# One layer's query projections moved into hyena as whole fp32 tiles, and four modulation blocks moved into the state chain

## What is computed

```python
def adaln(cond, w, b):                       # "modulation": 6 x 1024 outputs per layer
    return (silu(cond) @ w + b).reshape(cond.shape[0], 6, D_MODEL)

proj = u @ w_in                              # hy_in, s_z, s_xbc, s_dt, a_q, a_k, a_v, g
z = x1 * long_conv(v, filt[0]); hy = x2 * long_conv(z, filt[1])      # hyena: FFT convolutions
h = d * h + s                                # state-space branch: the chain of states over chunks
att = softmax(rope(q) @ rope(k).T + mask, sink) @ v                  # banded attention, 8 heads of 64
merged = sigmoid(g0)*(hy @ hy_proj) + sigmoid(g1)*(ssm @ ssm_proj) + sigmoid(g2)*(att @ attn_proj)
x = x + m2 * rmsnorm(merged @ w_out); x = x + m5 * rmsnorm(ffn(...))
```

## Time and profile before

| | |
|---|---|
| time, median of 3 runs | 2896.82 us (2895.7 to 2900.62) |
| the profiled execution's own time, its span | 2894.71 us, 2892.9 us |
| PE, PEld | 2675.1 us (92%), 2314.2 us (80%) |
| DVE, ACT, POOL | 1252.3 us (43%), 801.5 us (28%), 264.3 us (9%) |
| mean granted TensorE clock | 0.960 |
| chain that ended last, by engine | PE 81%, DVE 12%, ACT 4%, issue 2% |
| 1 MB weight load, issue to landing | 5.1 to 5.4 us, median of its kind |
| 64 KB load of a q block | 2.1 us |

### The profile page before, as it was taken

How to read it: one execution, slowest core, us unless ns; L and a number is a source line. 1 busy time by engine, 2 the same in 40 slices (tenths; PEclk the granted TensorE clock), 3 DMA queues, 4 the chain that set the end, 5 groups by cost and what they waited for, 6 DMA issues and landing times.

```text
span 2892.9 us, 38685 instructions
## 1 busy us (share of the span) xinstructions
PE 2675.1 (92%) x16849; PEld 2314.2 (80%) x16849; DVE 1252.3 (43%) x1978; ACT 801.5 (28%) x1234; POOL 264.3 (9%) x174
## 2 busy tenths in 40 slices
PE   6989897889999899999988998788999998999998
PEld 4946445679999799999977564385899988999997
DVE  3495646452233422223356756636422343223224
ACT  5222122352224522112252211224321244221212
POOL 0020412000111000000001204210001110000000
PEclk8989998899999999999999999988999999999999
DMA  6021003223323032323302010122232221222221
GB/s 241 19 78 44 29 15 90 73 75 117 96 81 102 17 104 88 103 93 98 91 30 78 4 59 15 44 75 75 80 124 89 83 78 41 77 66 81 69 88 41
DMA packets 214622, 213.42 MB, mean 74 GB/s; under 512 B 29480, under 2 KB 205040, under 8 KB 214070
## 3 DMA queue, kind: packets, MB, share of 16 engines
q1 hardware_dynamic: 214454, 210.95, 23.2%
HBM read 207.52 MB, written 3.41 MB: 73 GB/s over the span
## 4 chain that ended last, share of the span: by engine, by line
PE 81%; DVE 12%; ACT 4%; issue 2%; POOL 1%; DMA 1%; SPq 0%; DVEq 0%; ACTq 0%
PE ps L622 54%; PE ps L581 6%; DVE arena L1614 4%; PE ps L605 3%; PE ps L1100 3%; PE ps L593 3%; PE ps L672 1%; PE ps L882 1%; DVE arena L1715 1%; PE ps L1010 1%; ACT normed L723 1%; DVE normed L748 1%; PE ps L1165 1%; PE ps L1260 1%; ACT arena L2081 1%
## 5 line engine op out<-in xcount | busy, mean ns | idle before, releaser
L622 PE MATMUL ps<-arena_parts,weights_parts 128*128 128x320 f32 x8416 | 1428.9, 309 | 3.6 <-DVE normed_parts L1689 3.6
L622 PEld LDWEIGHTS ps<-arena_parts,weights_parts 128*128 128x128 f32 x8416 | 1275.8, 187 | 19.2 <-DVE normed_parts L1689 4.4
L539 DVE TENSOR_TENSOR weights_parts<-weights,weights_parts 128x2048 fp32r<-128x2048 f32 (+2 forms) x140 | 285.5, 2039 | 772.5 <-ACT weights_parts L531 772.5
L622 PE MATMUL ps<-normed_parts,weights_parts 128*128 128x320 f32 x2240 | 510.0, 309 | 0.0
L622 PEld LDWEIGHTS ps<-normed_parts,weights_parts 128*128 128x128 f32 x2240 | 376.1, 188 | 0.0
L531 ACT CAST weights_parts<-weights 128x2048 fp32r<-128x2048 f32 (+2 forms) x140 | 232.5, 1660 | 267.8 <-PE ps L622 171.5
L581 PE MATMUL ps<-normed,weights 128*128 128x320 f32 x768 | 214.9, 439 | 6.2 <-DVE arena L1597 5.5
L581 PEld LDWEIGHTS ps<-normed,weights 128*128 128x128 f32 x768 | 146.2, 192 | 77.2 <-issue 20.5
L605 PE MATMUL ps<-arena_parts 128*128 128x320 f32 x448 | 104.8, 340 | 51.8 <-DVE arena_parts L755 19.8
L605 PEld LDWEIGHTS ps<-arena_parts 128*128 128x128 f32 x448 | 81.1, 209 | 60.4 <-DVE arena_parts L755 27.4
L2280 POOL TENSOR_TENSOR arena<-arena 128x640 f32<-128x640 f32 x32 | 54.4, 1699 | 787.6 <-DVE arena L1789 783.2
(11 more groups left out here) (261 smaller groups left out, 2586.3 us busy)
## 6 DMA issues: line engine op xcount, KB each, us to landing
weights<-in_w_in_dram SPq DMA_DIRECT2D x48, 1024.0 KB, 5.3
weights<-in_ada_w_dram SPq DMA_DIRECT2D x40, 1024.0 KB, 5.4
weights<-in_ffn_w_gate_dram SPq DMA_DIRECT2D x22, 1024.0 KB, 5.3
weights<-in_ffn_w_up_dram SPq DMA_DIRECT2D x22, 1024.0 KB, 5.3
weights<-in_ffn_w_down_dram SPq DMA_DIRECT2D x24, 768.0 KB, 4.4
weights<-in_w_out_dram SPq DMA_DIRECT2D x8, 1024.0 KB, 5.1
weights<-in_w_in_dram SPq DMA_DIRECT2D x66, 64.0 KB, 2.1
arena<-in_ada_w_dram SPq DMA_DIRECT2D x2, 2048.0 KB, 15.5
```

The source lines that it names most:

```text
L539: Vc(dve.tensor_tensor(part_view(m, 1), raw_view(n), part_view(m, 0).bitcast(F32), ALU.subtract) .then_inc(vector_done, 1), "part", m)
L622: m = pe.matmul(tokens(s)[0:cols, lo:hi], a[:, k, oc], x[k][:, lo:hi], start=k == 0 and i == 0, stop=k == n - 1 and i == 2)
```

## The change

The query blocks are no longer split. q tile 0 is computed with `dense` right before the last transform tile of U, and tiles 1 to 3 between U and the inverse; attention begins with kT and vT. The four modulation blocks of that place (`IN_HYENA`, now `IN_CHAIN`) go into the state chain: rows before its odd steps, columns before its even ones, the last columns behind it. Their loads move in `blocks` ahead of the six hyena blocks. VectorE and ScalarE now split kv where they split q's first block. q lies in the two `act` buffers and two places of the arena, as hyena still holds the old place; vT, the rotation's buffers and the statistics take q's old place. `beside` is as it was.

```diff
-ADA_HY, ADA_ATT = 4, 6
+ADA_SSD, ADA_ATT = 4, 6
...
-    qT = tiled(arena, 7680, 4)
+    qT = [act[0], act[1], arena[:, 18944:18944 + T], arena[:, 19584:19584 + T]]
...
-    vT = arena[:, 19456:19456 + T]
+    vT = arena[:, 7680:7680 + T]
...
             w_in_block(("xbc", j), "parts", IN_XBC + QT * P * j)
         w_in_block(("dt",), "parts", IN_DT, 16)
+        for j in IN_CHAIN:
+            ada_block(l, j)
         for j in range(6):
             w_in_block(("hy", j), "whole", IN_HY + QT * P * j)
-        for j in IN_HYENA:
-            ada_block(l, j)
...
-    split_blocks = [n for n, blk in enumerate(blocks) if blk[1] != "whole"]
+    split_blocks = [n for n, blk in enumerate(blocks) if blk[1] not in ("whole", "q")]
...
                 for i, (c, r) in enumerate(CHAIN):
+                    if i % 2:
+                        ada_rows(pe, l, IN_CHAIN[i // 2])
+                    elif i:
+                        ada_columns(pe, l, IN_CHAIN[i // 2 - 1])
                     pe.wait_ge(vector_done, Vc["xw", c, r])
...
+                ada_columns(pe, l, IN_CHAIN[-1])
                 s = take(pe, "V", "end_rows")
...
+                def q_projection(o):
+
+                    w = weights(pe, l, "q", o // QT)
+                    s = take(pe, "S", "q", o, reuse=(l, "U", 1, "p") if o == 0 else (l, "U", 1, 0, ("cos", "sin")[o - 1]) if o < 3
+                             else (l, "q", 1))
+                    Tn(dense(pe, s, w, o % QT, hk).then_inc(tensor_done, 1), "q", o)
+                    if o % QT == QT - 1:
+                        w_used("q", o // QT)
...
                         for kind, rhs in (("cos", cos_rhs), ("sin", sin_rhs)):
-                            s = take(pe, engine, name, i, a, kind)
+                            last = (name, i, a, kind) == ("U", 1, 1, "sin")
+                            if last:
+                                q_projection(0)
+                            s = take(pe, engine, name, i, a, kind, reuse=(l, "q", 0) if last else None)
...
                 transform("U", 1, x1_tok, x1_tok, "V", False)
-                for j in IN_HYENA:
-                    ada_rows(pe, l, j)
-                    if j > IN_HYENA[0]:
-                        ada_columns(pe, l, j - 1)
-                ada_columns(pe, l, IN_HYENA[-1])
-
+                for o in range(1, 4):
+                    q_projection(o)
                 product_ready(1)
...
-                for o in range(4):
-                    if o % QT == 0:
-                        w = weight_parts(pe, "q", o // QT)
-                    s = take(pe, "S", "q", o)
-                    Tn(dense_parts(pe, s, w, o % QT, h2, after=None if o else h2_tile("att")).then_inc(tensor_done, 1), "q", o)
...
-                    Tn(dense_parts(pe, s, w, o, h2).then_inc(tensor_done, 1), *name)
+                    Tn(dense_parts(pe, s, w, o, h2, after=None if o else h2_tile("att")).then_inc(tensor_done, 1), *name)
...
                 for i, (c, r) in enumerate(CHAIN):
+                    if i and i % 2 == 0:
+                        later_modulation(l, IN_CHAIN[i // 2 - 1])
...
+                later_modulation(l, IN_CHAIN[-1])
                 dve.wait_ge(tensor_done, Tn["end_rows"])
...
                 spectrum(1)
-                for j in IN_HYENA:
-                    later_modulation(l, j)
-                split_lo(dve, split_index("q", 0))
+                split_lo(dve, split_index("kv"))
...
-                for m in range(split_index("q", 1), split_index("kv") + 1):
-                    split_lo(dve, m)
...
                 for c in range(NT):
+                    if c == 1:
+                        for j in IN_CHAIN:
+                            ada_rows(sc, l, j)
...
+                def q_kept(o):
+                    sc.wait_ge(tensor_done, Tn["q", o])
+                    Sc(sc.copy(qT[o] if o < 4 else kT, tokens(used("q", o))).then_inc(scalar_done, 1), "q", o)
...
                         for kind, dst in zip(("cos", "sin"), U_odd[a]):
+                            if (i, a, kind) == (1, 1, "sin"):
+                                q_kept(0)
...
-                for j in IN_HYENA:
-                    ada_rows(sc, l, j)
                 sc.wait_ge(pool_done, Gp["Y_mid", 1])
-                split_hi(sc, split_index("q", 0))
+                for o in range(1, 4):
+                    q_kept(o)
+                split_hi(sc, split_index("kv"))
...
-                for o in range(5):
-                    if o in (0, QT):
-                        split_hi(sc, split_index("q", o // QT) + 1)
-                    sc.wait_ge(tensor_done, Tn["q", o])
-                    Sc(sc.copy(qT[:, o, :] if o < 4 else kT, tokens(used("q", o))).then_inc(scalar_done, 1), "q", o)
+                q_kept(4)
```

More of the change, by code:

```diff
@@ L371, in programs @@
     PT_sb = [arena[:, 15104 + 1024 * i:15104 + 1024 * (i + 1)].rearrange("p (g n) -> p g n", g=2) for i in range(3)]
-    vT = arena[:, 19456:19456 + T]
-    rot_tmp = [arena[:, 18176 + 512 * i:18176 + 512 * (i + 1)] for i in range(2)]
-    stat = arena[:, 19200:19200 + 200].rearrange("p (n c) -> p n c", c=10)
+    vT = arena[:, 7680:7680 + T]
+    rot_tmp = [arena[:, 8320 + 512 * i:8320 + 512 * (i + 1)] for i in range(2)]
+    stat = arena[:, 9344:9344 + 200].rearrange("p (n c) -> p n c", c=10)
     merged = tiled(arena, 7680, 8)
@@ L403, in programs @@
     ADA_LATER = range(ADA_EARLY, 24)
-    IN_HYENA = [j for j in ADA_LATER][:ADA_HY]
-    IN_ATTENTION = [j for j in ADA_LATER][ADA_HY:ADA_HY + ADA_ATT]
-    IN_GATES = [j for j in ADA_LATER][ADA_HY + ADA_ATT:]
+    IN_CHAIN = [j for j in ADA_LATER][:ADA_SSD]
+    IN_ATTENTION = [j for j in ADA_LATER][ADA_SSD:ADA_SSD + ADA_ATT]
+    IN_GATES = [j for j in ADA_LATER][ADA_SSD + ADA_ATT:]
     ada_order = []
@@ L1198, in h2_tile @@
                     return lambda k: pe.wait_ge(vector_done, Vc["h_lo", name, k])
-                for o in range(4):
-                    if o % QT == 0:
-                        w = weight_parts(pe, "q", o // QT)
-                    s = take(pe, "S", "q", o)
-                    Tn(dense_parts(pe, s, w, o % QT, h2, after=None if o else h2_tile("att")).then_inc(tensor_done, 1), "q", o)
-                    if o % QT == QT - 1:
-                        w_used("q", o // QT)
                 w = weight_parts(pe, "kv")
@@ L1219, in _ @@
                     pe.wait_ge(scalar_done, Sc["q", o])
-                    src = (qT[:, o, :] if o < 4 else kT)
+                    src = qT[o] if o < 4 else kT
                     Tn(pe.matmul(slot(s)[:, 0:512], K("rotate"), src[:, LP:T], start=True, stop=True)
@@ L1231, in scores @@
                     for g in range(2):
-                        q = qT[64 * g:64 * g + 64, t, b * P:(b + 1) * P]
+                        q = qT[t][64 * g:64 * g + 64, b * P:(b + 1) * P]
                         if b == 0:
@@ L1690, in _ @@
                        .then_inc(vector_done, 1), "h_lo", "att", k)
-                for m in range(split_index("q", 1), split_index("kv") + 1):
-                    split_lo(dve, m)
                 for o in range(5):
-                    x = (qT[:, o, :] if o < 4 else kT)[:, LP:T]
+                    x = (qT[o] if o < 4 else kT)[:, LP:T]
                     dve.wait_ge(tensor_done, Tn["rot", o])
```

## The result

The changed kernel takes **2877.5 us** (median of 4 runs, 2874.66 to 2877.68) against 2896.26 for the kernel before beside it: 0.993, with a 95% interval of 0.9913 to 0.9947. It is 18.8 us faster. The forecast said 2889.1, 7.7 us faster; the sign was right and the size 11 us too small. The profiled execution took 2874.66 us, its span is 2872.9 (2892.9 before).

The account below looks back on a forecast made before the run. The prediction took TensorE to bound the kernel for most of the span. Layer 0 gave -7.1 + 2.5 = -4.6, layer 1 -5.6 + 2.5 = -3.1, together -7.7 from 2896.8 to 2889.1 us; range 2879 to 2902.

Parts of the forecast that it names:

- q0, the slot wait and U's last tile: Hyena's second half: first query tile 8.65 us, wait for ScalarE's copy 0.9, last transform tile 3.5.
- q1 to q3: Between U's last tile and the inverse: three whole fp32 query tiles at 8.65 us each, 25.95 us.
- The product is covered: Before the inverse: GpSimd's product ends between 468.2 and 473.8, before TensorE arrives at 475.1, so no wait.
- The inverse: Behind the query tiles: runs at the high clock throughout, 15.8 us instead of 17.4.
- The wait before the key tile: From inverse to kT: load, cast, split and hyY products in line, 14.9 us in layer 0, 16.4 in layer 1.
- The restart: At the kv tiles: TensorE restarts at the low clock for 6 us, 3.1 us lost; bounds nothing to 11.4.
- The chain: State chain with the modulation blocks added: +2.5 us per layer, of which +2 for the blocks.
- the store: End states' store queues behind tables and ScalarE waits for it before its third chunk: 0.5 us, bounds 0 to 3.
- Rival 1: The clock stays up through the chain (+0.5 for +2) and the restart costs half: 2882 us, chance 0.16.
- Rival 2: The kv load lands early and TensorE goes on 1.8 us after the inverse: 2857 us, chance 0.02.
- Rival 3: The low clock lasts through both kv tiles, 11.4 us lost instead of 3.1: 2906 us, chance 0.11.
- Rival 4: Chain at low clock throughout and ScalarE waits for the store, +4.3 + 3 per layer: 2898.7 us, chance 0.11.

Follow-up runs that it names:

- kv_early: The changed kernel with the two attention cache loads and SyncE's wait for the inverse moved behind the key and value load; 2844.89 us, ratio 0.9829.
- splits_behind: The changed kernel with only the key and value weights' splits moved behind ready work on ScalarE and VectorE; 2867.24 us, ratio 0.9905.
- chain_filler: The kernel before with one unused fp32 product of 512 columns in each state chain step but the first; 2891.93 us, ratio 0.9985.
- chain_alone: The kernel before with only the four modulation blocks moved into the state chain, queries still split and in place; 2897.49 us, ratio 1.0007.
- both: The changed kernel with kv_early's move and the first query tile put behind U's last transform tile; 2841.95 us, ratio 0.9817.
- chain_late_split: chain_alone with VectorE's split of the first query weights made to wait for GpSimd's last product; 2894.42 us, ratio 1.0000.

## Why the prediction was right in sign and too small

Step by step, layer 0 of the changed kernel against the sum:

- **q0, the slot wait and U's last tile** (forecast 8.65 + 0.9 + 3.5 = 13.05): 443.70 - 430.61 = 13.09. Right. **q1 to q3** (25.95): 25.85. Right, 8.62 a tile; the 9.4 us estimated from the Trainium skill's rule of four passes (FP8 and Floating Point Precision, TensorE Precision Notes) did not come.
- **The product is covered**: right. GpSimd was done at 464.9, 4.7 us ahead of the inverse.
- **The inverse** (15.8): 485.3 - 469.55 = 15.75. Right.
- **The wait before the key tile** (14.9 and 16.4): 14.7 in both layers. Its chain was right link by link, and kv_early and splits_behind show its two parts. Layer 1's slower landing (7.0 us in the earlier trace rows) did not come back; it landed in 5.4. I had taken one row's surplus for a property of the layer: 1.6 us.
- **The restart** (3.1): the step was mis-sized. From the key tile's start to the vT copy it is 16.0 us after and 14.4 in kv_early: 1.6 lost, 3.1 forecast. I had priced it from rows in which six full microseconds ran at the low clock; here it rose after some three. Two layers: 3.0 us.
- **The chain** (+2.5 per layer: +2 for the blocks, +0.5 for the store): the failed step, and the largest. The trace has -0.90 and -0.25, so 6.15 us of the missing gain lie here. The +2 was the middle between a low-clock price of +4.3, which adds TensorE's times up, and a high-clock price of +0.5. What came is -0.04 and +0.63 us from the first to the last state, and -0.86 and -0.88 in the end rows. So the low-clock price was too dear, since only some of the steps ran at that clock and a pair of them took 0.67 us more and not 1; and the forecast put at nothing what the blocks give back: TensorE, kept busy in the 1.00 us of each 2.12 in which it had waited for VectorE, was at the high clock when the end rows came (1.04 for 1.92). The shorter states (0.65 for 1.12) give nothing by themselves, as VectorE sets the pace. chain_filler shows the same with work that nobody needs. The store, priced at 0.5, made ScalarE wait 2.97 us, but the output stage kept its 40.7 us.

The chain's 6.15, the restart's 3.0 and the landing's 1.6 make 10.75 of the 10.8 us between -7.7 and -18.5; the medians differ by 0.3 more. Of the signs that the forecast named, two failed: the chain was not longer, and the clock was low for 3.3 us from the key tile's start and not for 6.

Rival 1, the clock stays up, was the case that came, with 0.16 and at 2882: it was right at the restart, which cost half, and half right in the chain, where the clock was at 1.00 in the second part of layer 0 and at the low level through the middle of layer 1. It too charged the chain +0.5 where it got shorter. Rival 2 did not come here, and describes what kv_early then did (2844.9, where 2857 was worked out). Rival 3 fell: behind 14.7 us of idle time the clock was back within 4 us. Rival 4 fell.

What the forecast did not see at all is how the parts hang together: that the queries alone, with the blocks behind them, would make the kernel 15 us slower, and the blocks' move alone would gain nothing.

## What to carry to other kernels

Work put where an engine waits for another costs nothing until it is longer than the wait. On TensorE price it at both clocks (here a pair of steps: nothing at the high one, 0.67 us at the low one), and look for TensorE's own work behind it on the path, which the higher clock makes shorter (here the end rows, 0.86 us). When the filling of a hole is exchanged, ask for each new tile how long it holds its weight place and what load now stands first behind it; here 14.5 us per layer hung on a wait that stood ahead of a load which did not need it. Where a load is late, put all work of the same engine that is ready ahead of its cast and split: that alone was 4.1 us per layer.

## What the runs showed of the hardware

- A restart of TensorE's clock in dense work cost 1.5 us, the same behind 14.7 us and behind 2.1 us of idle time (16.8 us for the two tiles, 15.2 without). Behind 1.81 us the clock stayed up in both layers of the kernel before, chain_alone, kv_early and both, and in layer 1 of chain_filler; it fell in both layers of chain_late_split and in layer 0 of chain_filler (45.0 for 43.5). What decides between these is open.
- GpSimd's step of 128 x 512 took 3.37 us beside a VectorE subtraction of 128 x 2048 and 1.26 without it. The profile shows no wait there, only a longer instruction.
- The 1 MB key load needed 5.3 and 5.4 us in the two layers of the changed kernel (486.2 to 491.5 in layer 0), but 7.0 in layer 1 of the kernel before; why is open.
- A VectorE-bound chain of states kept its 2.12 us a step whether TensorE's part took 1.12 or 0.65 us.
